# First level of a blocked triangular inverse: formed directly in the transposed layout, or transposed on TensorE

## The reference, cut to what matters

```python
k_beta = k * beta[..., None]
A = jnp.where(strict, jnp.einsum('bhnid,bhnjd->bhnij', k_beta, k) * decay, 0.0)
T = lax.linalg.triangular_solve(eye + A, jnp.broadcast_to(eye, A.shape), left_side=True, lower=True)
u = jnp.einsum('bhnij,bhnjd->bhnid', T, v * beta[..., None])
```

## Time and profile before

| | |
|---|---|
| median of 3 runs | 2994.56 us (2994.01 to 2999.91) |
| the profiled execution: own time, span | 2996.49 us, 2994.8 us |
| granted TensorE clock, mean | 0.993 |
| busy: PE, PEld | 2896.7 us (97%), 2401.6 us (80%) |
| busy: DVE, ACT, POOL | 1859.7 (62%), 1139.1 (38%), 1450.9 us (48%) |
| chunks of a half | about 314 to 611 us and 1747 to 2044 us |

### The profile page before, as it was taken

One profiled execution on the slowest core, in us unless ns is written; L12 is line 12 of the kernel. 1 busy time (PEld: TensorE's weight loads), 2 busy tenths in 40 slices (PEclk: granted clock), 3 DMA queues, 4 the chain that ended last, 5 costly groups with the idle time before them and its releaser, 6 DMA issues.

```text
span 2994.8 us, 42981 instructions
## 1 busy us (share of the span) xinstructions
PE 2896.7 (97%) x14070; PEld 2401.6 (80%) x14070; DVE 1859.7 (62%) x2616; ACT 1139.1 (38%) x2041; POOL 1450.9 (48%) x1192
## 2 busy tenths in 40 slices
PE   7999999999998999999989999999999899999997
PEld 7888788878887888887878878887888788888886
DVE  2564566656357777768866456665634866665767
ACT  4622444424234333334542244443423433333333
POOL 6422445452214555568972244444311455555896
PEclk9999999999999999999999999999999999999999
DMA  6623322141112444467642222214212122224764
GB/s 229 223 95 102 96 71 76 60 166 56 57 70 96 161 161 155 155 225 249 227 159 104 102 96 81 74 58 161 70 37 76 63 99 105 102 101 138 262 201 154
DMA packets 179208, 372.40 MB, mean 124 GB/s; under 512 B 17104, under 2 KB 58128, under 8 KB 179088
## 3 DMA queue, kind: packets, MB, share of 16 engines
q1 hardware_dynamic: 116592, 301.06, 29.2%
q10 hardware_dynamic: 62496, 69.78, 6.8%
HBM read 268.51 MB, written 102.27 MB: 124 GB/s over the span
## 4 chain that ended last, share of the span: by engine, by line
PE 83%; DVE 6%; POOL 4%; issue 4%; ACT 2%; DMA 1%; DVEq 0%; ACTq 0%; SPq 0%; POOLq 0%
PE PS L2797 19%; PE PS L2799 19%; PE PS L2798 19%; PE PS L1863 2%; PE PS L1862 2%; PE PS L1861 2%; PE PS L2832 2%; PE PS L2836 2%; PE PS L2834 2%; PE PS L1894 2%; PE PS L1890 2%; PE PS L1892 2%; PE PS L1774 1%; POOL sq_lo L627 1%; POOL am L661 1%
## 5 line engine op out<-in xcount | busy, mean ns | idle before, releaser
L2797 PE MATMUL PS<-act_hi,w_hi 128*128 128x512 f32 (+1 forms) x1088 | 429.6, 395 | 8.0 <-issue 4.0
L692 POOL TENSOR_TENSOR down_lo<-down_raw,down_hi 128x1024 fp32r<-128x1024 f32 x154 | 382.4, 2517 | 52.5 <-ACT down_hi L1154 52.5
L2799 PE MATMUL PS<-act_hi,w_lo 128*128 128x512 f32 (+1 forms) x1088 | 407.4, 374 | 0.0
L2798 PE MATMUL PS<-act_lo,w_hi 128*128 128x512 f32 (+1 forms) x1088 | 406.4, 374 | 0.0
L2241 POOL TENSOR_TENSOR w_lo<-raw,w_hi 128x256 fp32r<-128x256 f32 (+1 forms) x144 | 195.2, 1378 | 423.0 <-ACT w_hi L2317 423.0
L1604 DVE TENSOR_TENSOR copied<-copied,PS 128x512 f32<-128x512 f32 x308 | 207.3, 685 | 244.3 <-PE PS L2799 234.1
L685 POOL TENSOR_TENSOR part_lo<-sum_s,part_hi 128x512 fp32r<-128x512 f32 x176 | 233.5, 1333 | 232.8 <-ACT part_hi L1134 232.2
L2797 PE MATMUL PS<-op_t_hi,part_hi 128*128 128x512 f32 x704 | 275.5, 391 | 0.0
L2798 PE MATMUL PS<-op_t_lo,part_hi 128*128 128x512 f32 x704 | 274.8, 390 | 0.0
L2799 PE MATMUL PS<-op_t_hi,part_lo 128*128 128x512 f32 x704 | 274.8, 390 | 0.0
L1154 ACT ACTIVATE down_hi<-down_raw 128x1024 fp32r<-128x1024 f32 x154 | 159.5, 1057 | 237.7 <-PE PS L2799 123.8
(11 more groups left out here) (332 smaller groups left out, 6400.7 us busy)
## 6 DMA issues: line engine op xcount, KB each, us to landing
raw<-in_w_units SPq DMA_DIRECT2D x132, 512.0 KB, 3.8
a_d<-copied SPq DMA_DIRECT2D x154, 256.0 KB, 2.2
down_raw<-a_d SPq DMA_DIRECT2D x154, 256.0 KB, 3.6
gu_raw<-in_w_units SPq DMA_DIRECT2D x44, 512.0 KB, 4.7
down_raw<-t_d SPq DMA_DIRECT2D x88, 256.0 KB, 3.0
down_raw<-in_w_units SPq DMA_DIRECT2D x66, 256.0 KB, 3.0
qkvz_d<-stage ACTq DMA_DIRECT2D x64, 256.0 KB, 2.5
raw<-att_d SPq DMA_DIRECT2D x32, 512.0 KB, 3.3
```

Source lines behind the costliest of these rows:

```text
L692: pool.tensor_tensor(flat(lo[:, :, :]), flat(down_raw[m % 4][:, :, :]), flat(hi[:, :, :]).bitcast(f32), ALU.subtract)\
L2797: nc.tensor.matmul(out_ap, whi, xhi, start=start, stop=False)
L2798: nc.tensor.matmul(out_ap, whi, xlo, start=False, stop=False)
L2799: return nc.tensor.matmul(out_ap, wlo, xhi, start=False, stop=stop)
```

## The change

The pairs' entries are formed directly where the transpose has them. Since the Gram product is symmetric, its odd columns with the other half of the decay tile (`dec[:, 1]`, which is the decay transposed) give the transposed entries. But beta belongs to the row of A, which is now the column's neighbour, so a tile `next_beta` is made that holds for each token the beta of the next one, by a product with a shifted identity once a half. POOL forms am0 with half the elements in two products (mask, then next_beta), DVE multiplies in the Gram product's odd columns, copies the identity's even columns into Xm and writes its odd columns as identity minus am0. The step keeps its place in the list and its fill under the name inv, and TensorE does nothing in it.

```diff
 def decays_pool(pool, n, m, par):
     pool.wait_ge(S["dec_ready"], n + 1)
+    pool.wait_ge(S["x_ready"], n * LEVELS)
+    pool.tensor_tensor(am0[:, :, :], odd_columns(dec[par][:, 1, :, :]),
+                       first_mask[:, :].unsqueeze(1).broadcast_to([P, NH, P // 2]),
+                       ALU.mult).then_inc(S["decm_ready"], 1)
+    pool.wait_ge(S["decm_ready"], n * 4 + 1)
+    pool.tensor_tensor(am0[:, :, :], am0[:, :, :],
+                       next_beta[:, bass.ds(m, 1), :].rearrange("p n h -> p (n h)")
+                       .unsqueeze(2).broadcast_to([P, NH, P // 2]),
+                       ALU.mult).then_inc(S["decm_ready"], 1)
     pool.tensor_tensor(dec[par][:, 0, :, :], dec[par][:, 0, :, :], gate("beta", m),
-                       ALU.mult).then_inc(S["decm_ready"], 1)
-    pool.wait_ge(S["decm_ready"], n * 3 + 1)
-    pool.wait_ge(S["a1t_full"], n)
-    pool.tensor_tensor(am0[:, :, :], dec[par][:, 0, :, :], over_heads(first_mask[:, :]),
                        ALU.mult).then_inc(S["decm_ready"], 1)
     pool.tensor_tensor(dec[par][:, 1, :, :], dec[par][:, 1, :, :], over_heads(upto[:, :]),
                        ALU.mult).then_inc(S["decm_ready"], 1)
...
 # POOL, before level 2's masked piece
-    pool.wait_ge(S["a1t_full"], n + 1)
+    pool.wait_ge(S["x_ready"], n * LEVELS + 1)
...
 # DVE, step gram
-    dve.wait_ge(S["decm_ready"], n * 3 + 3)
-    dve.tensor_tensor(two(am0[:, :, :]), gram[:, :, :, 0, :], two(am0[:, :, :]),
+    dve.wait_ge(S["decm_ready"], n * 4 + 4)
+    dve.tensor_tensor(two(am0[:, :, :]),
+                      gram.rearrange("p b h s (m e) -> p b h s m e", e=2)
+                      [:, :, :, 0, :, 1], two(am0[:, :, :]),
                       ALU.mult).then_inc(S["am0_ready"], 1)
...
 # DVE, step a1t, now inv
-    dve.wait_ge(S["a1t_full"], n + 1)
-    dve.tensor_tensor(Xm[:, :, :], over_heads(ident[:, :]), r4(bank(2)),
-                      ALU.subtract).then_inc(S["x_ready"], 1)
+    dve.wait_ge(S["am0_ready"], n + 1)
+    dve.tensor_copy(even_only(Xm[:, :, :]), ident_half(0))
+    dve.tensor_tensor(odd_columns(Xm[:, :, :]), ident_half(1),
+                      am0[:, :, :], ALU.subtract).then_inc(S["x_ready"], 1)
...
 # TensorE
-if step == "a1t":
-    pe.wait_ge(S["am0_ready"], n + 1)
-    pe.wait_ge(S["scln_ready"], R * 2 if par == 1 or first else R * 2 - 1)
-    for hh in range(NH):
-        t = nc.tensor.transpose(r4(bank(2))[:, hh, :], am0[:, hh, :], ident[:, :])
-    t.then_inc(S["a1t_full"], 1)
 if step[0] == "y":
     pe.wait_ge(S["x_ready"], n * LEVELS + l)
     pe.wait_ge(S["am_ready"], n * 6 + l)
     if l == 1:
+        pe.wait_ge(S["scln_ready"], R * 2 if par == 1 or first else R * 2 - 1)
         pe.wait_ge(S["vb_ready"], n + 1)
...
 # once a half: TensorE's gc_sums and DVE's gates
+nc.tensor.matmul(PS[0:P - 1, 7, 2 * TT * NH:3 * TT * NH], ident[:, 1:P],
+                 flat(G["beta"][:, :, :]), start=True, stop=True)
...
+step("bc", lambda: dve.tensor_copy(next_beta[:, :, :], g["beta"]))
+step("bs", lambda: dve.tensor_copy(flat(next_beta[0:P - 1, :, :]),
+                                   PS[0:P - 1, 7, 2 * TT * NH:3 * TT * NH]))
...
-pe.wait_ge(S["gate_step_dve"], half * GATE_DVE + GD["g"])
+pe.wait_ge(S["gate_step_dve"], half * GATE_DVE + GD["b2"])
```

More of the change, by code:

```diff
@@ L103 @@
 GD = {n: i + 1 for i, n in enumerate(
-    "copy sum a neg min bmin w1 wm eq mx rc l1 l2 l3 sp g b1 b2 gc gl fd nb nn".split())}
+    "copy sum a neg min bmin w1 wm eq mx rc l1 l2 l3 sp g b1 b2 gc gl bc bs fd nb nn".split())}
 GATE_DVE = len(GD)
@@ L137 @@
 PREP_RAW = ["raw_ready0", "raw_ready1", "prep_raw2", "prep_raw3"]
-STEPS = ["load", "start", "gram", "a1t"] + [f"{x}{l}" for l in range(1, LEVELS) for x in "yx"] + list("wvo")
+STEPS = ["load", "start", "gram", "inv"] + [f"{x}{l}" for l in range(1, LEVELS) for x in "yx"] + list("wvo")
 FILL = [0, 0, 2, 2] + [2, 1] * 6 + [2, 0, 0]
@@ L179, in block_kernel @@
         upto = sb("upto", [P, P])
-        first_mask = sb("first_mask", [P, P])
+        first_mask = sb("first_mask", [P, P // 2])
+        cursor[0] += P // 2 * 4
         even_mask = sb("even_mask", [P, LEVELS - 1, P // 2])
@@ L256, in block_kernel @@
         dec = [sb("dec0", [P, 2, NH, P], at=z), sb("dec1", [P, 2, NH, P], at=[slot3])]
-        am0 = sb("am0", [P, NH, P], at=z)
+        am0 = sb("am0", [P, NH, P // 2], at=z)
+        z[0] += NH * P // 2 * 4
         am = sb("am", [P, 2, NH, P // 2], at=z)
@@ L264, in block_kernel @@
         Tm = sb("Tm", [P, 2, P], at=z)
+        next_beta = sb("next_beta", [P, TT, NH], at=[z[0]])
         z[0] += NH * P * 4
@@ L360, in block_kernel @@
              "o_stored")
-        sems("gc_full nrm_full kt_full vt_full gram_full a1t_full y_full xy_full xt_full ks_full "
+        sems("gc_full nrm_full kt_full vt_full gram_full y_full xy_full xt_full ks_full "
              "vn_full o_full kv_full ont_full")
@@ L631, in squares_lo, with odd_columns, even_only, ident_half @@
             last.then_inc(S["sql_ready"], 1)
+        def odd_columns(ap):
+            return ap.rearrange("p h (m e) -> p h m e", e=2)[:, :, :, 1]
+        def even_only(ap):
+            return ap.rearrange("p h (m e) -> p h m e", e=2)[:, :, :, 0]
+        def ident_half(e):
+            return ident[:, :].rearrange("p (m e) -> p m e", e=2)[:, :, e].unsqueeze(1)                .broadcast_to([P, NH, P // 2])
         def decays_pool(pool, n, m, par):
             pool.wait_ge(S["dec_ready"], n + 1)
+            pool.wait_ge(S["x_ready"], n * LEVELS)
[7 more added lines that the diff above has]
+                               ALU.mult).then_inc(S["decm_ready"], 1)
             pool.tensor_tensor(dec[par][:, 0, :, :], dec[par][:, 0, :, :], gate("beta", m),
-                               ALU.mult).then_inc(S["decm_ready"], 1)
-            pool.wait_ge(S["decm_ready"], n * 3 + 1)
-            pool.wait_ge(S["a1t_full"], n)
-            pool.tensor_tensor(am0[:, :, :], dec[par][:, 0, :, :], over_heads(first_mask[:, :]),
                                ALU.mult).then_inc(S["decm_ready"], 1)
@@ L1395, in chunk_dve @@
                                       ALU.mult).then_inc(S["a_ready"], 1)
-                if step == "a1t":
+                if step == "inv":
                     if first:
@@ L2197, in build_masks @@
                     m = P // (2 * b)
[L2198 to L2201, removed]
+                    v = (even_mask[:, l - 1, :] if l else first_mask[:, :])\
+                        .rearrange("p (m c) -> p m c", c=b)
+                    first, last = (b, 2 * b - 1) if l else (0, 0)
                     pool.wait_ge(made(), n)
@@ L2205, in build_masks @@
                     pool.wait_ge(made(), n)
-                    triangle(v, -b, [[-2 * b, m], [0, b]], 1)
+                    triangle(v, -first, [[-2 * b, m], [0, b]], 1)
                     n += 1
                     pool.wait_ge(made(), n)
-                    triangle(v, 2 * b - 1, [[2 * b, m], [0, b]], -1)
+                    triangle(v, last, [[2 * b, m], [0, b]], -1)
                     n += 1
```

## The result

| | before | after |
|---|---|---|
| median | 2994.50 us (22 runs, 2990.97 to 2999.91) | 2999.64 us (22 runs, 2994.74 to 3003.07) |
| the profiled execution: own time, span | 2996.49 us, 2994.8 us | 2998.86 us, 2997.1 us |
| granted TensorE clock, mean | 0.993 | 0.992 |

The ratio after to before is 1.0014, with a 95% interval of 1.0008 to 1.0020: about 4 us slower, where 3.4 us faster was forecast.

A forecast was written before the change was run, and what follows sets the result against it. TensorE's nearly full instruction stream (97% busy) was taken as the bound. Gain 4.3, less 0.2 for POOL's pieces and 0.7 for the gates, gave 3.4 us: 2991.2 us, range 2987.5 to 2995.5.

The forecast's parts named there:

- a price on this lock, one place earlier: Identity copy into Xm held until POOL's first mask product ends: ready at s+2.39 held, s+2.15 undisturbed.
- gained 0.10 there: Chunk 0, level-1 product's load: at 335.67 us instead of 335.77, as Xm is ready slightly sooner.
- The gain term, 4.3 us: Four transposes fewer in 16 chunks, limited by when Xm is ready: 2.14 us per half, bounds 0 to 7.0.
- s: Start of DVE's am0 product in a chunk, from which the prediction counted the times until Xm is ready.
- The 0.44 us of the slots: TensorE's stream loses 0.44 us per chunk when the four transposes' load slots go.
- nothing elsewhere: POOL's four mask and decay pieces instead of three: no loss outside each half's chunk 0.
- The 0.1 us that POOL's four pieces were to cost in each chunk 0: Normalisation in each chunk 0, reshuffled by POOL's pieces: 0.1 us lost each, 0.2 in all.
- The 0.7 us for the gates' product: Once per half, one added product with the shifted identity: 2 x 0.34 = 0.7 us, hidden by nothing.
- the slower rival: Loop chunks: L1283 falls behind one more POOL product, some 15 us less 3.4, giving 3006 us; chance 6%.
- the 7.0 us of slots: Upper bound through TensorE's stream for leaving out the transposes: 16 chunks x 0.44 us.

The follow-up runs named there:

- the run with the wait on xe_ready: The changed kernel, but POOL's masked product of level 2 waits for the copy Xe of level 1, not for Xm: 2995.48 us, ratio 0.9997.
- its three variants: The kernel before with only the gates' part (2994.52 us), only the later level-2 product (2998.59 us), or the four am0 transposes made twice (3002.80 us).
- transposes twice: The kernel before with the four transposes of am0 made twice in every chunk: 3002.80 us, ratio 1.0025.

## Why the prediction was wrong

**The step that failed** is "The second mask product now waits for Xm instead of the transposes; it is needed a level later, some 2 us on: nothing." It looked at when the product is needed and not at what else Xm releases. POOL's product and Xe's copy now start together, in chunks 1 to 6 POOL is first, and the copy takes 0.83 us instead of 0.29 or 0.44, in front of TensorE. It cost 1.1 us a half (the run with the wait on xe_ready), and in the kernel before the same wait cost 0.6 to 0.9. The prediction had even put a price on this lock, one place earlier. The Trainium skill, page "SBUF — State Buffer", section "Who interferes with whom", says that whichever of the two issues first has the shared ports for its whole instruction; the starts at 441.44 and 441.49 and the end 0.15 after POOL's agree. So do chunks 0 and 7, where DVE is first by 0.04 us, its copy runs free and POOL's product takes 0.84 us (chunk 7) instead of 0.73.

**What it did not look at** is the clock. It counted the time that TensorE would wait in chunk 0 and gained 0.10 there; measured from the Gram product, L1794 came 0.16 us earlier (4.41 instead of 4.57), as forecast. But without the transposes TensorE stands still for 2.22 us in one piece instead of 1.95 in two, and behind that the clock fell in four of the six halves profiled of the changed kernel, at 1.1 to 1.3 us each. The kernel before had no fall there in the eight halves profiled of it and its three variants.

**The gain term, 4.3 us**, was right in size once the failed step is undone. For the seven distances of a half it says 2.14, less 0.44 for chunk 7: 1.70. The run with POOL after Xe measured 242.62-241.28 = 1.34 and 242.81-241.29 = 1.52. For chunk 7 it says 0.44, and 0.3 was measured. Its parts, for chunk 3 of the changed kernel: the held copy ends at s+2.10 (2.06 forecast) and Xm is ready at s+2.43 (2.39), L1794 is loaded at s+2.64 (2.60). The 0.44 us of the slots holds too (transposes twice), save in chunk 0. Chunk 2 gained 0.23 at L1794 instead of 0.32 (5.29 us behind the Gram product instead of 5.52), since the load followed Xm by 0.31 and not by 0.21.

**Chunks 3 and 5** were to gain 0.10 and lost 0.07 at L1794 in the first half (5.59 instead of 5.52), because s itself came 0.13 later; in the second half L1794 came at 5.79 and 5.73. The rows show DVE's ost_t ending with a POOL piece of the decays, 1.10 us after the Gram product's load instead of 0.96, and the state's update, for which the transposes of v wait, behind it: 0.58 us of waiting instead of 0.44. The prediction said "nothing elsewhere" of the four POOL pieces. That the shifted pieces do this is read from the rows; no run isolated it.

**The additions.** The 0.1 us that POOL's four pieces were to cost in each chunk 0 measured 0.17: TensorE's wait for kqn ahead of the Gram product, outside the distances, grew in both halves. Before and after:

```profile
330.81 0.42 PEld L1741 LDWEIGHTS PS<-ident,kqn 128*128 128x128 f32 x4 [1.71 <-DVE kqn L1283]
```

```profile
332.35 0.42 PEld L1767 LDWEIGHTS PS<-ident,kqn 128*128 128x128 f32 x4 [1.88 <-DVE kqn L1306]
```

The 0.7 us for the gates' product can't be seen in a time. L1283 (now L1306) was held longer, as the slower rival had it, but TensorE hardly waits more for it (5.6 us of all before, 6.0 now). The two rows, before and after:

```profile
L1283 DVE SCALAR_TENSOR_TENSOR kqn<-qk,rn 128x512 f32<-128x512 f32 x16 | 17.3, 1083 | 0.0
```

```profile
L1306 DVE SCALAR_TENSOR_TENSOR kqn<-qk,rn 128x512 f32<-128x512 f32 x16 | 23.3, 1457 | 0.0
```

That rival gave the right sign by the wrong mechanism.

**What stays open** is part of the size. At full clock the edit gains 0.7 us in the distances and 0.6 in the two chunks 7, and loses 0.3 ahead of the two chunks 0: 1.0 us. Four falls in six halves are 1.3 per run, at 1.1 to 1.3 us each 1.5 to 1.7 us. That leaves the chunks 0.5 to 0.7 us slower, 1.4 at most with the 0.7 us forecast for the gates. The ratio 1.0014 (1.0008 to 1.0020) is 2.4 to 6.0 us.

The timed runs seem to have had more falls than the profiled ones. One fall, 3.41 us long in the clock records of the traces, takes 3.41 x 0.5/2995 = 0.00057 off the mean clock. The changed kernel's mean was lower by 0.99303-0.99218 = 0.00085 in one job and by 0.0011 in another, which is 1.5 and 1.9 falls a run, or 1.6 to 2.5 us. There the mean times differ by 2999.47-2996.99 = 2.5 us and by 2998.18-2995.09 = 3.1. Less the gain of 1.0 us, the falls explain 0.6 to 1.5 of these, and 1.5 to 2 us are left.

The profiles show no more of the lower level outside chunk 0 than before. Without the stretch at the program's end, the time at the lower level outside chunk 0 adds up to 27.3, 30.7 and 23.9 us in the three profiles of the changed kernel, and to 27.3 (before), 30.7, 30.7 and 34.1 in the four that lack the edit in their chunks. Two falls a run would fit into the two chunks 0, but only the profiled executions show where theirs were. So the lock is shown by runs from both sides, and the falls are seen in the traces, each with its price. Together they turn the gain into a small loss. Why the timed runs lose 1.5 to 2 us more is open, and part of it may be scatter.

## What to carry to other kernels

When a wait is moved to another semaphore, list everything that this semaphore releases: two engines that start on the same signal can run one behind the other, as POOL and DVE did here, and the one on the critical path may be second; which is first was settled by 0.05 us. Where an edit takes instructions out of a wait of TensorE, look at the granted clock behind the wait: idle time of 1.95 us in two pieces had no fall here, 2.2 us in one piece had one in half of the cases. And an edit that frees slots is only worth what its operand gains: here ACT had to write the identity ahead of time, and two orders had to change, before the 7.0 us of slots turned into 5 us of time (2989.83 against 2994.87).

## What was not expected of the hardware

- With one semaphore releasing both, POOL began 0.05 us before DVE's copy in every chunk of the loop and held it: 0.83 us for a copy of 128x256 that takes 0.29 alone. In the chunks written out DVE began 0.04 us before POOL, and the copy took 0.29.
- The granted clock went to its lower level for some 3.4 us behind waits of 1.9 to 2.65 us, in 8 of 14 cases, at 1.1 to 1.3 us of time each, in the middle of a stretch in which TensorE was otherwise 97% busy.
- The same kernel, with the same wait of 2.2 us, had the fall in both halves in two profiled executions and in none of a third.
